# A drain on GpSimd, a later T1 copy, and T4's transfer ahead of T3's in the fifth layer

## What is computed

```python
def swiglu(x, w_gu, w_down):
    gate, up = jnp.split(x @ w_gu, 2, axis=-1)
    return (jax.nn.silu(gate) * up) @ w_down

# second_block, the end of its last layer
h = h + rmsnorm_2(mix, g[3])
h = h + 0.5 * rmsnorm_2(swiglu(rmsnorm_2(h, g[4]), ffn_w_gu[l, 1], ffn_w_down[l, 1]), g[5])
```

## Time and profile before

| what | value |
|---|---|
| median of 3 runs | 1259.68 us (1259.24 to 1260.21) |
| profiled execution | 1259.1 us |
| its span, first to last instruction | 1257.3 us |
| PE busy | 1245.9 us, 99% |
| DVE busy | 1033.6 us, 82% |
| ACT busy | 803.8 us, 64% |
| GpSimd busy | 181.1 us, 14% |
| moved by DMA | 282.57 MB, mean 225 GB/s |

### The profile page before, as it was taken

How to read it: one execution, slowest core, us unless ns; L and a number is a source line. 1 busy time by engine, 2 the same in 40 slices (tenths; PEclk the granted TensorE clock), 3 DMA queues, 4 the chain that set the end, 5 groups by cost and what they waited for, 6 DMA issues and landing times.

```text
span 1257.3 us, 15589 instructions
## 1 busy us (share of the span) xinstructions
PE 1245.9 (99%) x5893; PEld 1029.1 (82%) x5893; DVE 1033.6 (82%) x1043; ACT 803.8 (64%) x988; POOL 181.1 (14%) x222
## 2 busy tenths in 40 slices
PE   9999999999999999999999999999999999999997
PEld 7888888888888888888888888888888878778886
DVE  6776689999789997767899997899977568999984
ACT  6675576666576665645666665776657467866662
POOL 6142130110011100102311100211001003301100
PEclk9999999999999999999999999999999999999999
DMA  9537499997659955568999978599655536999830
GB/s 331 181 101 235 133 328 290 269 271 247 195 170 273 272 172 182 198 222 210 348 281 250 267 261 238 151 262 275 198 175 199 179 101 203 312 322 273 245 135 34
DMA packets 136763, 282.57 MB, mean 225 GB/s; under 512 B 9152, under 2 KB 40056, under 8 KB 136688
## 3 DMA queue, kind: packets, MB, share of 16 engines
q1 hardware_dynamic: 120192, 229.67, 51.7%
q0 software_dynamic: 16048, 50.79, 21.6%
q10 hardware_dynamic: 448, 1.12, 0.3%
HBM read 243.79 MB, written 1.05 MB: 195 GB/s over the span
## 4 chain that ended last, share of the span: by engine, by line
PE 91%; DMA 3%; DVE 2%; issue 1%; ACT 1%; POOL 1%; DVEq 0%; POOLq 0%; ACTq 0%
PE B L2151 17%; PE B L2153 17%; PE B L2152 17%; PE B L2606 8%; PE B L2608 8%; PE B L2607 8%; PE T L2151 4%; PE T L2153 4%; PE T L2152 4%; DMA KT<-in_ffn_w_gu 2%; PE T L2630 1%; DMA QT<-VD 1%; DVE w_lo L1398 1%; PE B L2145 1%; PE T L2145 0%
## 5 line engine op out<-in xcount | busy, mean ns | idle before, releaser
L1398 DVE TENSOR_TENSOR w_lo<-w_raw,w_hi 128x2048 fp32r<-128x2048 f32 x129 | 296.3, 2299 | 76.1 <-ACT w_hi L799 75.8
L799 ACT ACTIVATE w_hi<-w_raw 128x2048 fp32r<-128x2048 f32 x129 | 247.2, 1918 | 93.6 <-PE B L2608 54.9
L2151 PE MATMUL B<-w_hi,xt_lo 128*128 128x512 f32 x652 | 259.8, 399 | 1.0 <-DVE xt_lo L1730 0.6
L2153 PE MATMUL B<-w_hi,xt_hi 128*128 128x512 f32 x652 | 254.6, 390 | 0.0
L2152 PE MATMUL B<-w_lo,xt_hi 128*128 128x512 f32 x652 | 254.1, 390 | 0.0
L2606 PE MATMUL B<-w_hi,act_lo 128*128 128x512 f32 x440 | 172.8, 393 | 0.8 <-DVE act_lo L1854 0.7
L2608 PE MATMUL B<-w_hi,act_hi 128*128 128x512 f32 x440 | 171.4, 390 | 0.0
L2607 PE MATMUL B<-w_lo,act_hi 128*128 128x512 f32 x440 | 171.3, 389 | 0.0
L2151 PEld LDWEIGHTS B<-w_hi,xt_lo 128*128 128x128 f32 x652 | 122.5, 188 | 30.0 <-issue 3.0
L2153 PEld LDWEIGHTS B<-w_hi,xt_hi 128*128 128x128 f32 x652 | 122.4, 188 | 26.1
L2152 PEld LDWEIGHTS B<-w_lo,xt_hi 128*128 128x128 f32 x652 | 122.6, 188 | 23.3
(11 more groups left out here) (332 smaller groups left out, 2113.7 us busy)
## 6 DMA issues: line engine op xcount, KB each, us to landing
w_raw<-in_ffn_w_down SPq DMA_DIRECT2D x88, 512.0 KB, 5.7
Z<-in_ffn_w_gu SPq DMA_DIRECT2D x64, 512.0 KB, 8.1
w_raw<-in_ffn_w_gu SPq DMA_DIRECT2D x48, 512.0 KB, 5.5
Z<-nat POOLq DMA_DIRECT2D x40, 512.0 KB, 8.0
nat<-in_ffn_w_gu SPq DMA_DIRECT2D x32, 512.0 KB, 7.7
QT<-in_ffn_w_gu SPq DMA_DIRECT2D x32, 512.0 KB, 7.0
w_raw<-in_conv_w_in SPq DMA_DIRECT2D x24, 512.0 KB, 4.8
w_raw<-in_w_down SPq DMA_DIRECT2D x22, 512.0 KB, 6.4
```

Of the source, the lines that this page charges most:

```text
L799: act.activation(whi[home(u)][:, :], raw[slot][:, :], ACT.Copy).then_inc(w_hi, 1)
L1398: dve.tensor_tensor(wlo[home(u)][:, :], src, whi[home(u)][:, :].bitcast(F32), ALU.subtract).then_inc(w_lo, 1)
L2151: pe.matmul(bank[:, :], lo[:, k, x], whi[s][:, c], start=first, stop=False, skip_group_check=more)
L2153: return pe.matmul(bank[:, :], hi[:, k, x], whi[s][:, c], start=False, stop=last, skip_group_check=more)
```

## The change

Two functions get the layer as an argument; GpSimd gets a drain before the last statistic; in add_blocks the transfer of the first pair's T4 is issued for p = 0 (before T3) in the layer f = 4, where it was issued for p = 1; and copy_t1(4) on ACT is moved behind xt_hi of the second token tile, ahead of the split of N1a. A sum of T4 for the first pair is added to DVE's list for the case that over_b21 is false.

```diff
-def over_b21(p):
+def over_b21(f, p):
     return p == 0
 def sums_of(f):
-    return (((0, "T1"), (0, "T2")) if f % 2 else ()) + SUMS
+    return (((0, "T1"), (0, "T2")) if f % 2 else ()) + (() if over_b21(f, 0) else ((0, "T4"),)) + SUMS
...
-        def operand(name, p):
+        def operand(name, f, p):
...
             def add_blocks(f, p0=0):
                 for p in range(p0, SQUARES):
-                    if p == 1:
+                    if p == (0 if f == 4 else 1):
                         first_t4(f)
                     add_block("T3", f, p)
                     if p in ADDED_T4:
...
             row_stat("h8")
             add_blocks(4)
+            pool.drain()
             row_stat("y5")
...
                     turned_hi(reader, lambda k: gain + k, 1)
+                    if f == 4:
+                        act.wait_ge(at_v, D_R + DIFF_H)
+                        copy_t1(4)
                     if f != 1:
                         split_at(u0 + 2)
...
-                    elif src == "T4" and p == 0:
+                    elif src == "T4" and over_b21(f, p):
                         act.wait_ge(t4_first, 32 * f + 32)
...
             sum_squares("y4", "ffn4", U_O + 3, (), n2(1, 4), AO, early=8)
-            act.wait_ge(at_v, D_R + DIFF_H)
-            copy_t1(4)
             ffn(4, "h8", "ffn4", n2(1, 4), k0=8)
...
                     dve.wait_ge(b_in["B11"], 32 * (n + 1))
+                elif name == "T4" and p == 0 and f % 2 == 0:
+                    dve.wait_ge(t2_in, 16 * f + 32)
                 else:
...
                 block("P3", 0)
+                if not over_b21(f, 0):
+                    weight_sum("T4", f, 0)
                 block("P7", 0)
```

More of the change, by code:

```diff
@@ L262, in build @@
         OPERAND = {"P1": "B11", "P2": "B21", "P3": "B22", "P4": "T4", "P5": "T1", "P6": "T2", "P7": "T3"}
-        def operand(name, p):
+        def operand(name, f, p):
             src = OPERAND[name]
-            if src == "T4" and over_b21(p):
+            if src == "T4" and over_b21(f, p):
                 return WB["B21"]
@@ L1101, in block @@
                     src = OPERAND[name]
-                    place = operand(name, p)
+                    place = operand(name, f, p)
                     if src in WB:
@@ L1813, in block @@
                 def block(name, p):
-                    lo_of(u0 + OP[name, p], operand(name, p))
+                    lo_of(u0 + OP[name, p], operand(name, f, p))
                 def next_sum(name):
```

## The result

The changed kernel takes 1265.28 us (median of four runs, 1264.91 to 1266.15), where the kernel before took 1259.46 us on the same chip (four runs, 1258.71 to 1260.21). The ratio is 1.0048, with an interval of 1.0037 to 1.006. So the change costs 5.8 us; 9.5 were forecast. The profiled execution took 1264.91 us, and its span grew by the same 5.8 us, from 1257.3 to 1263.1.

What follows compares the result with a forecast made beforehand. PE, busy 99% of the span at full clock, was taken as the bound. 8.6 - 0.9 + 1.8 = +9.5 us on 1259.1 gave 1268.6, and 0.6 for the median gave 1269.2 us; range 1263.0 to 1274.0.

Steps and rivals of the forecast that it cites:

- The edits that do nothing: over_b21 still returns p == 0, so sums_of, the new weight_sum on DVE and operand change nothing: cost 0, gain 0.
- T4's order: On GpSimd, T4 still waits for P2's low part and goes out at 1100.2, T3 behind it at 1101.9.
- P7's delay, +8.6: At P7 in the last layer, T3 complete at 1115.1 makes P7 ready at 1119.3, so PE is 8.6 us late.
- rival 2: Slower GpSimd queue, halves 4.25 us apart: T3 at 1117.7, P7 at 1121.9, total 1273.5 us; chance 0.12.
- rival 3: Faster queue, T4 costs T3 nothing: T3 at 1110.6, P7 at 1114.8, +3.2, total 1262.9 us; chance 0.11.
- The readiness of P7, 4.2 us after T3: On ACT and DVE, splitting P7's operand and its low part take 4.2 us from T3's landing to P7 ready.
- N1a, +1.2 inside the stall: The later T1 copy makes N1a 1.2 us late, contained in PE's standstill in front of P7.
- D1, -0.9: Between P7 and D1, D1 finds its operand about when PE arrives: 0.9 us back, bounded by -0.1.
- The clock, +1.8: After PE's idle time ahead of P7, the slower clock costs 1.8 us, with 0 below and 2.7 above.
- Rival 1: At P7 the stall comes but PE's clock holds: +7.7, total 1267.4 us; chance 0.15.
- The drain, 0: GpSimd's drain before the last statistic is covered by 61.25 us of idle time and gains nothing: 0.
- rival 4: Not slower: halves pass side by side, T3's second half needs 3.9 us or less, P7 stays covered, 1259.0 us; chance 0.07.

Runs made afterwards that it cites:

- the copy alone: The kernel before with only copy_t1(4) and its wait moved behind xt_hi, no drain, T3 first: 1260.21 us, ratio 1.001.
- T4 first with the drain: The kernel before with the drain and T4's transfer ahead of T3's, the T1 copy at its old place: 1265.3 us, ratio 1.005.
- the run with products in the gap: The changed kernel with twenty unread 128 x 128 products on PE right behind the first pair's P3: 1262.6 us, ratio 1.0031 to the kernel before.

## Why the prediction was right or wrong

The forecast was 1269.2 us in a range of 1263.0 to 1274.0, slower; measured were 1265.28, slower. The direction, the place and the mechanism at P7 held. Two terms there had the wrong size, and a third, the drain, was put at nothing without a row for it.

- **The edits that do nothing, and T4's order.** Right. T4 was issued at 1100.50 (1100.2 forecast) and T3 at 1101.67 (1101.9).
- **P7's delay, +8.6: mis-sized, it was +6.7.** The step that failed is "I take 3.3, the spacing of these same two transfers in this same stage". That spacing was measured with Sync's loads beside it (29% of the engines from 1104 to 1107, 99% from 1110 to 1112), and the text itself says, at rival 2, that Sync is held back by T3 here. With q1 quiet the halves came 2.4 to 2.5 us apart. The first one after 5.0 was right (5.1). T3 was complete after 12.5 us, not 14.9, between the forecast and rival 3.
- **The readiness of P7, 4.2 us after T3.** Right in size (4.3 from 1113.0), but misread: in the kernel before the 4.2 count from ACT's start at 1105.98, and T3 had landed at 1105.3, ahead of a pass of 0.6 us that ACT had to do first. Now ACT stands waiting for T3, and those 0.7 us aren't there.
- **N1a, +1.2 inside the stall.** Right: +1.13 in the kernel after, +1.4 alone without the stall (the copy alone), and nothing beside it (T4 first with the drain took the time of the whole change). One thing was missed: the prediction lets T3 land later because T4 is issued 1.2 us later, but with T4 issued 1.9 us earlier T3 still came in at 1113, in part because Sync's loads held T4 until 1101 either way.
- **D1, -0.9.** Right to the tenth, and its wait is gone; with the clock held up P7 to D1 took 10.97 us, 0.8 less than before.
- **The clock, +1.8: it was +2.3 to 2.4.** The value is the loss of another piece of work: sixteen small matmuls that take 1.95 us at the full pace, where P7's twelve take 2.72. The upper bound, all twelve at twice 0.227, was nearer: they followed at 0.43, the last at 0.31. Rival 1, the clock holds, fell, and the run with products in the gap shows what it would have been worth.
- **The drain, 0: wrong, it was -2.4 in the profile and -2.2 in the runs.** The steps that failed are "No row shows a drain" and "It can't gain either: nothing slow stands behind it". The trace of before has the closing drain of 6.76 us behind the statistic, and Sync's last wait of 2.6 us. The statistic was taken for the last thing on GpSimd. The sum from the last statistic to the end would have told it: 1257.3 - 1250.3 = 7.0 us, of which the outputs needed 4.3.
- **Rivals 2 and 4 fell.** The halves came closer together than forecast, not further apart, and T3's second half took 10.8 us where rival 4 needed 3.9. By the fit in the Trainium skill, DMA: Bandwidth & Descriptors, section on the anatomy of one DMA, one half is estimated at 3.2 us; the rows here have 5.1 for the first and 2.4 to 2.5 from one to the next, so for these sums, which read and write SBUF, the measurement disagrees.

The time came nearer to rival 3's 1262.9 than its reason deserved: about 1.9 us of the difference to the forecast are the pace of the queue, 2.4 the drain, and the clock took 0.6 back.

## What to carry to other kernels

An operand that is issued behind another transfer on a queue in order is late by that transfer's wait plus its bytes; compute it with the pace of the queue as it will be loaded then, and ask which loads the change itself holds back. When PE must stand still for several microseconds, add the slow clock behind the gap at its full price; here it held for nearly all of the next unit and cost 2.3 us. And read the end of the kernel past its last instruction: here the closing drain of GpSimd, which had issued 117 transfers, ended last, and an earlier drain, where the engine was idle, took it out.

## What the runs showed of the hardware that was not expected

GpSimd's closing drain took 0.66, 2.38, 3.73 and 6.76 us with 0, 21, 58 and 117 transfers issued since the one before, all of them landed. A first drain in the middle took 5.5 us at 525.9 (59 transfers before it), 6.0 at 971.3 (96) and 11.9 to 12.0 right behind the last transfer, which takes up to 8.0 us to land. And a sum from SBUF to SBUF moves 0.20 MB per us with all 16 engines at 105%, where Sync's loads move 0.39 to 0.40 at the same share.
